# A mixture-of-experts layer on one core: the experts' output goes into a transposed residual in SBUF, column by column, in place of rows scattered to memory

## The reference

```python
h = rmsnorm(x, g_moe)                       # 512 x 1024
top_val, top_idx = top_k(h @ w_router + b_router, 4)      # 32 experts
gate = softmax(top_val)
# for each token and each of its 4 experts e:
hc  = h[tok] @ w1[e] + b1[e]                # 1024 -> 2048
act = glu * sigmoid(1.702 * glu) * (lin + 1)
y   = act @ w2[e] + b2[e]                   # 1024 -> 1024
out[tok] += gate * y
x = x + out
return rmsnorm(x, g_final)
```

## Time and profile before

| | us |
|---|---|
| median of three runs | 1723.14 |
| profiled execution, whole | 1722.98 |
| its span, first to last instruction | 1721.3 |
| PE busy | 1642.4 (95%) |
| DVE / ACT / POOL busy | 579.2 / 480.6 / 218.8 |
| DMA, mean over the span | 293 GB/s, 505.08 MB |

### The profile page before, as it was taken

One profiled execution on the slowest core, in us unless ns is written; L12 is line 12 of the kernel. 1 busy time (PEld: TensorE's weight loads), 2 busy tenths in 40 slices (PEclk: granted clock), 3 DMA queues, 4 the chain that ended last, 5 costly groups with the idle time before them and its releaser, 6 DMA issues.

```text
span 1721.3 us, 41456 instructions
## 1 busy us (share of the span) xinstructions
PE 1642.4 (95%) x15736; PEld 933.8 (54%) x15736; DVE 579.2 (34%) x1893; ACT 480.6 (28%) x1534; POOL 218.8 (13%) x719
## 2 busy tenths in 40 slices
PE   7989999999999999799999999999999999999985
PEld 6756887788889858534343434343434334333341
DVE  4344525534645351652132213221312122131115
ACT  5465332443325342312121212121211212112111
POOL 0011301000000001012121202220211112012010
PEclk9999999999999999999999999999999999999998
DMA  7202634324225506699999999999999999999996
GB/s 249 74 25 57 218 130 170 101 88 158 98 98 177 201 14 245 228 398 374 416 417 420 419 419 419 421 418 420 419 420 419 420 420 420 420 420 419 419 401 268
DMA packets 97419, 505.08 MB, mean 293 GB/s; under 512 B 9744, under 2 KB 9928, under 8 KB 47760
## 3 DMA queue, kind: packets, MB, share of 16 engines
q1 hardware_dynamic: 87808, 473.99, 68.8%
q0 software_dynamic: 8880, 26.70, 4.6%
q10 hardware_dynamic: 576, 2.10, 0.3%
HBM read 477.86 MB, written 25.03 MB: 292 GB/s over the span
## 4 chain that ended last, share of the span: by engine, by line
PE 73%; SPq 14%; DMA 7%; DVE 2%; issue 2%; ACT 1%; POOL 0%; DVEq 0%; POOLq 0%; ACTq 0%; another core or an unknown queue 0%
PE ps L2060 20%; SPq L547 13%; PE ps L2086 11%; PE ps L1711 10%; PE ps L1712 10%; PE ps L1713 10%; DMA ring<-in_w_exp_in 3%; DMA ring<-in_w_exp_out 2%; PE ps L1807 1%; DMA ring<-y_tok 1%; PE ps L1854 1%; PE ps L1874 1%; PE ps L2023 1%; DMA r_rows<-work 1%; PE ps L515 1%
## 5 line engine op out<-in xcount | busy, mean ns | idle before, releaser
L2060 PE MATMUL ps<-ring,moe 128*32 128x512 f32 x3104 | 344.2, 593 | 14.7 <-DMA ring<-in_w_exp_in 14.7
L1575 DVE TENSOR_SCALAR moe<-ps 128x768 f32<-128x768 f32 (+1 forms) x32 | 26.7, 833 | 609.3 <-PE ps L2060 609.3
L2060 PEld LDWEIGHTS ps<-ring,moe 128*32 128x32 f32 x3104 | 94.2, 110 | 247.4 <-issue 203.9
L1167 DVE TENSOR_TENSOR wl<-raw,wh 128x1024 fp32r<-128x1024 f32 x102 | 123.5, 1223 | 231.6 <-ACT wh L812 231.6
L2086 PE MATMUL ps<-ring,moe 128*32 128x256 f32 x3136 | 174.7, 379 | 0.5 <-DMA ring<-in_w_exp_out 0.3
L812 ACT ACTIVATE wh<-raw 128x1024 fp32r<-128x1024 f32 x102 | 106.9, 1060 | 224.0 <-PE ps L1713 224.0
L1711 PE MATMUL ps<-oph,wh 128*128 128x512 f32 x384 | 151.7, 395 | 4.6 <-DVE opl L1202 2.2
L1712 PE MATMUL ps<-opl,wh 128*128 128x512 f32 x384 | 150.7, 392 | 0.0
L527 DVE COPY moe<-work 128x8 f32 x960 | 127.8, 180 | 67.6 <-issue 66.7
L1713 PE MATMUL ps<-oph,wl 128*128 128x512 f32 x384 | 150.5, 392 | 0.0
L1079 ACT ACTIVATE moe<-ps 128x768 f32<-128x768 f32 (+1 forms) x32 | 22.8, 711 | 453.6 <-DVE moe L1575 453.6
(11 more groups left out here) (310 smaller groups left out, 1929.7 us busy)
## 6 DMA issues: line engine op xcount, KB each, us to landing
ring<-in_w_exp_in SPq DMA_DIRECT2D x152, 1024.0 KB
ring<-in_w_exp_out SPq DMA_DIRECT2D x78, 1024.0 KB
moe<-in_w_exp_in SPq DMA_DIRECT2D x52, 1024.0 KB
work<-in_w_exp_in SPq DMA_DIRECT2D x52, 1024.0 KB
moe<-in_w_exp_out SPq DMA_DIRECT2D x26, 1024.0 KB
raw<-in_w_in SPq DMA_DIRECT2D x25, 1024.0 KB
work<-in_w_exp_out SPq DMA_DIRECT2D x24, 1024.0 KB
y_tok<-spare POOLq DMA_DIRECT2D x16, 512.0 KB, 4.1
```

The source lines that it names most:

```text
L1167: nc.vector.tensor_tensor(half_lo(g), raw[:, g // 2 % RAW, g % 2 * PC:(g % 2 + 1) * PC], half_hi(g), ALU.subtract).then_inc(w_lo, 1)
L1575: nc.vector.tensor_scalar(act_n[:, 0:g], ps[:, 0:g, 256:512].rearrange("p j (n a) -> p j a n", a=2), 1.0 - LIMIT, 1.0 + LIMIT, ALU.max, AL ...
L2060: ins = nc.tensor.matmul(ps[32 * s:32 * s + 32, j, :], xt[:, k, 32 * j:32 * j + 32], w[:, s, :, :], start=False, stop=(k == KT - 1), tile_ ...
```

## The change

`acc_t`, the residual in transposed form (8 x 512 values in each partition), stays in `work` at 4096 to 8191. ACT writes it while it copies out the router's transposes of `res`, which are made in either version. The two weight places there go: `SLOTS` is 18, and the chunks 17 and 18 now wait for the first expert's gather (`xt_made`). `h_rows`, `r_rows`, `y_tok`, their stores and loads, the gather and the scatters are gone. The gain of the norm is applied by ACT when it writes columns, no longer by DVE to the rows.

For each expert: `y_evict` multiplies by the gate (one instruction for each group); PE transposes the result in `y_turn`, inside the `up` of two steps later, after its first chunk, through banks 6 and 7; ACT keeps it (`y_cols_keep`); DVE adds its 96 or 64 columns, each to `acc_t[:, :, token]`, ahead of `swiglu(p)`. Empty rows are filled with tokens that the expert does not have, at gate 0. ACT and POOL share the token copies half and half (48 or 32 each); DVE has none. At the end PE transposes `acc_t` back into PSUM, adds the last expert's rows there, and ACT and DVE normalise from PSUM.

```diff
-SLOTS = FIRST + 4
+SLOTS = FIRST + 2
-TURN = 5
+TURN = 3
@@ SP
                 elif s == FIRST:
-                    sp.wait_ge(nat_ready, TT)
-                    sp.wait_ge(lg_done, 1)
-                elif s == FIRST + 2:
-                    sp.wait_ge(h_stored, 16 * TT)
-                    sp.wait_ge(xt_made, 1)
+                    sp.wait_ge(xt_made, 2)
-                if s in (13, 15):
...
-                    sp.dma_start(r_rows[:, :, 512 * half:512 * half + 512], res[:, :, 512 * half:512 * half + 512]).then_inc(res_moved, 16)
+            for q in range(2, W2):
+                refill(0, W1 + q, down_chunk(0, q))
...
-            sp.dma_start(res, r_rows).then_inc(res_moved, 16)
-            sp.wait_ge(w_used, DP + down_chunk(NE - 2, W2))
-            sp.wait_ge(y_stored, scattered(NE - 1))
-            for u in range(TT * TOPK):
-                sp.dma_start(y_rows[u], y_tiles[u // TOPK, u % TOPK]).then_inc(row_in[u], 16)
@@ POOL
-                if CYCLE[i] > 2:
-                    copy_tokens(mybir.EngineType.Pool, nc.gpsimd.tensor_copy, i, LOW, CAP).then_inc(x_pool, 1)
+                pool.wait_ge(row_ready, p + 3)
+                pool.sem_inc(bias_turn, 1)
+                copy_part(i, CYCLE[i])
-            def scatter(n, g):
...
@@ ACT
-            act.wait_ge(res_moved, 32)
             for k in range(KT - 2):
                 column_tile(k)
...
-                if g > 2:
-                    nc.scalar.activation(y_sb[:, 2, :], ps[:, 5, 0:256], ACT.Copy)
-                nc.scalar.activation(y_sb[:, 0:2, :], ps[:, 4, :].rearrange("p (j n) -> p j n", j=2), ACT.Copy).then_inc(y_kept, 1)
+                for j in range(g):
+                    a = j % 2 * 256
+                    ins = nc.scalar.activation(y_sb[:, j, :], ps[:, 4 + j // 2, a:a + 256], ACT.Copy, scale=gate_now[:, j:j + 1])
+                ins.then_inc(y_kept, 1)
...
+            def y_cols_keep(n, g):
+                act.wait_ge(yt_made, n + 1)
+                act.wait_ge(acc_done, n)
+                act.sem_inc(bias_turn, 1)
+                nc.scalar.activation(y_cols[:, 0:g * 256].rearrange("p (h n) -> p h n", h=2), ps[:, 6:8, 0:g * P], ACT.Copy).then_inc(yt_kept, 1)
@@ DVE
-                nc.vector.scalar_tensor_tensor(h_nat[:, t, :], res[:, t, :], rstd[:, t:t + 1], g_moe_b,
-                                               ALU.mult, ALU.mult).then_inc(nat_ready, 1)
+                nc.vector.tensor_scalar(h_nat[:, t, :], res[:, t, :], rstd[:, t:t + 1], None, ALU.mult).then_inc(nat_ready, 1)
...
+            def add_columns(row, g, lo, hi, step=None):
+                columns = y_cols[:, 0:g * 256].rearrange("p (h j s n) -> p s h j n", h=2, j=g, s=4)
+                for s in range(lo, hi, 8):
+                    for i, token in enumerate(load_tokens(mybir.EngineType.DVE, row, s)):
...
+                        at = acc_t[:, :, bass.ds(token, 1)].rearrange("p (s h) n -> p s h n", h=2)
+                        j, n = divmod(s + i, 32)
+                        ins = nc.vector.tensor_tensor(at, at, columns[:, :, :, j, n:n + 1], ALU.add)
...
+            def add_rows(n, g, b):
+                dve.wait_ge(row_kept, n + 1)
+                dve.wait_ge(yt_kept, n + 1)
+                dve.wait_ge(acc_done, n)
+                dve.sem_inc(bias_turn, 1)
+                add_columns(tok_acc[b], g, 0, 32 * g).then_inc(acc_done, 1)
...
-            def turn(p, i, g, stores):
+            def turn(p, i, done, g):
+                add_rows(p - 2, done, i)
                 swiglu(p, CYCLE[i], p * EC + UPS)
-                index(p + 2, CYCLE[i], i, row=True)
+                keep_row(p, CYCLE[i], i)
+                index(p + 2, CYCLE[i], i, rows=p + 1)
                 e = expert_at(p + 3)
                 choose_with(e, e, CYCLE[1 - i])
-                now(p - 1, g, stores)
-                copy_part(p + 2, i)
+                now(p - 1, g, p - 1)
@@ DVE, the end
+            add_rows(NE - 3, CYCLE[1], 1)
...
+            add_columns(tok_acc[0], CYCLE[0], 0, LOW)
             swiglu(NE - 1, CYCLE[1], DP + up_chunk(NE - 1, W1))
+            add_columns(tok_acc[0], CYCLE[0], LOW, CAP).then_inc(acc_done, 1)
@@ PE
+            def y_turn(n, g, ats, ys):
+                pe.wait_ge(at_kept, ats)
+                pe.wait_ge(y_kept, ys)
+                for h in range(2):
+                    for j in range(g):
+                        ins = nc.tensor.transpose(ps[:, 6 + h, j * P:(j + 1) * P], y_sb[:, j, h * P:(h + 1) * P], ident)
+                ins.then_inc(yt_made, 1)
...
-                up(p, CYCLE[i], p * 2 + 1)
+                up(p, CYCLE[i], p * 2 + 1, between={0: lambda: y_turn(p - 2, older, p, p - 1)})
...
-                act_turn(p, CYCLE[i])
+                act_turn(p, CYCLE[i], p - 1)
...
+            up(NE - 1, CYCLE[1], 2 * NE - 1, between={1: rows_turn})
+            act_turn(NE - 1, CYCLE[1], NE - 1)
+            last_down({t: lambda t=t: tile_back(t) for t in range(TT - 1)})
+            tile_back(TT - 1)
+            for t in range(TT):
+                own_rows(t).then_inc(own_done, 1)
```

More of the change, by code:

```diff
@@ L57 @@
 AHEAD = 5
-ROWS = 8
 W1 = KT
@@ L300, in layer_kernel @@
         g_moe_c = small[:, 0:8]
-        logit_t = work[:, 6656:7168]
+        logit_t = spare[:, 256:768]
         ss_more = xmax
@@ new lines, in _ @@
+            chain.wait()
+            dve.wait_ge(pick_ready, 1)
+            chain(nc.vector.tensor_scalar(slots[:, :, 0:NE], slot, -1.0, None, ALU.add))
+            dve.wait_ge(gate_exp, 4)
+            chain(nc.vector.reciprocal(names["grec"], names["gsum"]))
+            chain.wait()
+            chain(nc.vector.tensor_tensor(gate, gate, names["grec"].unsqueeze(2).to_broadcast([P, TT, TOPK]), ALU.mult))
+            chain.wait()
+            chain(nc.vector.tensor_tensor(oh2, oh, gate.unsqueeze(3).to_broadcast([P, TT, TOPK, NE]), ALU.mult))
@@ L1519, in _ @@
             for j in range(1, BLK):
-                chain(nc.vector.scalar_tensor_tensor(slots[:, :, j * NE:(j + 1) * NE], sel, 4.0 * T, slot, ALU.mult, ALU.add))
-            chain.wait()
-            for j in range(1, BLK):
-                v = slots[:, :, j * NE:(j + 1) * NE]
-                chain(nc.vector.tensor_scalar(v, v, -1.0 - CAP * j - 4.0 * T, None, ALU.add))
+                chain(nc.vector.tensor_scalar(slots[:, :, j * NE:(j + 1) * NE], slot, -1.0 - CAP * j, None, ALU.add))
             chain.wait()
@@ L1952, in _ @@
             ins.then_inc(lg_done, 1)
-            def keep_running(n):
-                for _ in range(n):
-                    nc.tensor.matmul(ps[:, 3, 0:P], ident, ident, start=True, stop=True, skip_group_check=True)
             def column_turn(k):
@@ L1973, in _, with index @@
             ins.then_inc(rank_done, 1)
-            def index(n, g, row=False):
+            def index(n, g, first=False):
                 pe.wait_ge(pick_ready, n + 2)
-                pe.wait_ge(found_out, n)
-                if row:
-                    if n > 2:
-                        pe.wait_ge(row_ready, n - 2)
-                    for t in range(TT):
-                        for c in range(2):
-                            nc.tensor.matmul(ps[0:1, 3, 64:64 + 32 * g], column[:, t, c, 0:1], pick[:, t, 0:32 * g],
-                                             start=(t == 0 and c == 0), stop=(t == TT - 1 and c == 1), skip_group_check=True)
+                if not first:
+                    pe.wait_ge(found_out, n)
+                    pe.wait_ge(row_ready, n)
+                for t in range(TT):
+                    for c in range(2):
+                        nc.tensor.matmul(ps[0:1, 3, 64:64 + 32 * g], column[:, t, c, 0:1], pick[:, t, 0:32 * g],
+                                         start=(t == 0 and c == 0), stop=(t == TT - 1 and c == 1), skip_group_check=True)
                 for t in range(TT):
@@ L2089, in down, with last_down @@
                     ins.then_inc(w_used, 1)
-            def last_down():
+            def last_down(between={}):
                 pe.wait_ge(at_kept, NE)
@@ L2155, in _ @@
                                            start=(t == 0), stop=(t == TT - 1))
-            ins.then_inc(xt_made, 1)
+                if k % 4 == 3:
+                    ins.then_inc(xt_made, 1)
             pe.wait_ge(b_hi, 3)
             pe.wait_ge(ht_out, 2 * KT)
-            index(0, groups(0))
-            up(0, groups(0), 1, first=True, between={1: lambda: index(1, groups(1))}, kept=1)
-            x_turn(1)
-            index(2, CYCLE[0], row=True)
-            act_turn(0, groups(0), 2)
@@ L2164, in _ @@
-            up(1, groups(1), 3, kept=2)
+            pe.wait_ge(tok_ready, 1)
+            up(0, groups(0), 1, first=True, between={0: lambda: index(0, groups(0), first=True), 3: lambda: index(1, groups(1))})
+            index(2, CYCLE[0])
+            act_turn(0, groups(0))
+            up(1, groups(1), 3)
             spread(0, groups(0), 0, 3, 0)
-            index(3, CYCLE[1], row=True)
+            index(3, CYCLE[1])
```

(10 more changed lines are left out.)

560 lines of the change are left out of this document (225 added, 335 removed).

## The result

The changed kernel takes 1741.86 us (median of four runs, 1739.7 to 1746.78) against 1722.57 us before (four runs as well): the ratio is 1.0111, 95% interval 1.0097 to 1.0125. The forecast was 1698 us. The profiled execution has a span of 1744.9 us, 23.6 more than before.

A forecast was written before the change was run, and what follows sets the result against it. The prediction took the expert loop as a race, PE eating the lead of loaded chunks, then DMA pacing from about 1270 us. Terms -5.1 + 12.2 - 19.6 - 3.5 - 9.2 = -25.2 gave span 1696.1, time 1698 us, range 1691 to 1703 (50%).

The forecast's parts named there:

- Transfers: Weight loads in the expert loop: DMA needs 60.1 us a pair without scatters, 1.45 more than PE; lead 24 us.
- signs of being wrong: Expert loop: adds' batches over 1.86 us, PE waiting for weights before 1600, or pairs staying at 60 us or more.
- the end: After the last `up`: 37.8 us to the end of the span in place of 47.0, a gain of 9.2 us.
- The hand-over: From routing to the first expert: no store of `res`, gather 5.9 us earlier; net -5.1 us, first weight product about 714.
- Rival 3: The hand-over gives nothing, as copies of expert 1's columns or another gather wait hold it up: +5, 1703 us; 10%.
- `y_turn`: PE's added transposes in each `up`: a pair becomes 58.65 us; +12.2 us up to the end of `up(18)`.
- DVE's adds: DVE's column adds ahead of `swiglu`: 0.205 us a column, hidden by `down` up to 0.232 in three-group steps.
- Rival 2: DVE paces the loop: adds at 0.2485 us a column give 1724 us, at 0.262 1744 us; 15%.
- The lead: Weight chunks loaded ahead at the first expert: worth 24 us in place of 34; PE should just not run dry.
- Rival 1: DMA still paces the loop, as scatters cost only their bytes: 60.8 us a pair, 1705 to 1710 us; 18%.

The follow-up runs named there:

- e5: e4 with the loop's first instruction 64 places behind a block's start in place of at it: 1740.11 us, ratio 1.0096 to the kernel before.
- e4: Changed kernel, all adds kept, with 16 tokens a read in place of 8 and VectorE's loop put at a block's start: 1704.32 us, ratio 0.9878.
- e2: Changed kernel with every second add of VectorE left out, all token reads kept: 1697.20 us, ratio 0.9845 to the kernel before.
- e8: e4 with the chunk of one place in eighteen loaded as two transfers, of 120 and 8 partitions: 1846.58 us, ratio 1.0703.

## Why the prediction was wrong, by its own steps

**The step that failed is *Transfers*: "Without scatters the DMA engines need 60.1 us for a pair".** It took the 419 GB/s of the earlier trace rows for a property of the transfers and put it beside a new program. In these runs the rate held only while all sixteen engines had queued work. VectorE's body went from 180 to 392 instructions, and queue 14 began to fetch it, 5 packets of 8 KB a pair, and one engine fell behind with them. Between 940 and 1070 us the 16th landing fell behind the 15th by (22.1 - 6.1) - (9.5 - 3.0) = 9.5 us, 7.3 in 100, while 11 packets came: 0.9 us for each fetch, where the packet itself lasts 0.325 us. Once the lead of the others is used up, all go at the pace of the late one: 418 less 7.3% is 388 GB/s, and 392 was measured. 25.17 MB at 392 take 64.2 us; the pairs took 64.9, where the prediction had 60.1 for DMA and 58.65 for PE. Two of its own signs of being wrong came: PE waits for weights before 1600 (from 1177 us on), and pairs stay over 60 us.

The share of 1.01 in the earlier trace rows hid the risk, and the prediction priced the adds by VectorE's time alone. How many instructions a loop has is a cost of its own, and it was nowhere among the terms, nor in the rivals. The profile of the kernel before shows that such fetches exist, 29 packets on queue 14 in the whole run, and that its loop causes none; what a longer body would do can't be read there. The Trainium skill, Runtime: NRT & Kernel Launch, section "Instruction fetch mechanics", says that instruction memories are refilled by DMA in 16 KiB blocks, that the cost of crossing a block's boundary is mostly hidden, and that a taken branch to a block no longer held forces a fetch and stalls the engine. That a loop's body is fetched again agrees with the runs. The block does not: queue 14's packets are of 8 KB. Nor does the place of the cost: it lies on the DMA engine that carries the fetches (35.8 us between e5 and e4). VectorE itself pauses for 0.3 us within a batch of adds, 3 us ahead of the next packet (rows below), and e4's loop has no such pause; its slack hides them, for up to 1157 us a pair takes 58.9 us in both kernels.

**The other terms, read in e4**, where the fetches are gone (spans 1702.7 against 1721.3: -18.6, forecast -25.2):

| stretch | forecast | e4 | changed kernel |
|---|---|---|---|
| to the end of `up(18)` | -5.1 + 12.2 = +7.1 | +12.2 (1275.54 against 1263.37) | +18.9 |
| `up(18)` to `up(30)` | -19.6 | -17.7 (353.8 us) | +15.0 (386.6 us) |
| `up(30)` to `up(31)` | -3.5 | -2.7 | -2.5 |
| the end | -9.2 | -10.3 (36.6 us) | -7.8 (39.1 us) |
| sum | -25.2 | -18.5 | +23.6 |

- *The hand-over* was right in kind and too small. The first weight product starts at 713.0 us in the changed kernel and 713.5 in e4, against 720.99; 714 was forecast. Rival 3 is refuted.
- *`y_turn`*: 58.96 a pair in e4, 58.65 forecast.
- *DVE's adds* were priced right. In the changed kernel, in order of time:

```profile
1049.09 1.08 DVE L1429 TENSOR_TENSOR work<-work,spare 128x8 f32 x8 [5.18 <-issue]
1050.75 1.08 DVE L1429 TENSOR_TENSOR work<-work,spare 128x8 f32 x8 [0.58 <-issue]
1052.42 0.43 DVE L1429 TENSOR_TENSOR work<-work,spare 128x8 f32 x3 [0.58 <-issue]
1053.15 0.69 DVE L1429 TENSOR_TENSOR work<-work,spare 128x8 f32 x5 [0.30 <-issue]
...
1057.77 1.08 DVE L1429 TENSOR_TENSOR work<-work,spare 128x8 f32 x8 [0.59 <-issue]
1059.43 1.08 DVE L1429 TENSOR_TENSOR work<-work,spare 128x8 f32 x8 [0.59 <-issue]
```

1.66 us a batch, 0.208 a column (0.205 forecast, margin 0.232), with one address computation each; eight adds of 0.176 us lie within 1.08 us, so they overlap as the copies do. The batch in two parts, 3 and 5 with 0.30 us between, is one of the pauses; queue 14's next packet comes at 1056.2. Rival 2 is refuted as the cause in the loop. That its upper case, 1744 us, lies beside the measured 1741.86 is chance: it wanted 0.262 us a column. The rival holds in one place that the sum passed over: the steps of experts 2 and 3 follow experts of three groups both, so 96 columns stand ahead of a two-group step too. PE waits there 2.0 us for `swiglu`, and the end of `up(4)` is level with before (863.51 against 862.6), though the first product was 7.5 us earlier. Half the adds (e2) end `up(4)` at 858.0. Those 5.5 us are about what is missing in the first row of the table (5.1), and most of the 7.1 us between e2 and e4; that they are the same microseconds is argued from their size.
- *The lead* lasted: e4 never waits for weights, with 18 places and DMA at 419. The estimate "just not dry" stands; in its DMA arithmetic only the rate was wrong for the changed kernel.
- *The end*: 36.6 us in e4 for 37.8 forecast.
- *Rival 1* (DMA still paces) named the right resource and a wrong reason, too little saved by the scatters' going, and so 1705 to 1710. e4 refutes the reason: its transfers are those of the changed kernel, and PE never waits for them.

With the failed step mended the kernel is at 1704.3, one us outside the forecast's own range of 1691 to 1703, and faster than before, as forecast.

## What to carry to other kernels

When a change adds instructions to a loop, count the body against the instruction store before pricing them by their time (here three blocks of 128 for VectorE), and look in the profile whether an instruction queue moves packets inside the loop. If it does, shorten the body or put its start at a block's start. When DMA paces a kernel and its rate is a few per cent under what it was, compare the landings of one transfer: if one of the sixteen is always last, the mean share of the engines says nothing of the one that counts.

## What the runs showed of the hardware that was not expected

- VectorE's loop body of 382 instructions causes no fetches in the loop when it begins at a block's start, and 5 fetches of 8 KB in each pass when it begins 64 places later (e4, e5); 392 instructions cause them in either place; bodies of 180 and 232 don't where they happened to lie.
- One fetch of 8 KB sets its DMA engine back by about 0.9 us (an estimate from 9.5 us for 11 packets), three times the packet's own 0.325 us.
- In these kernels one DMA engine came to be 20 to 22 us behind the first before the rate suffered. In the changed kernel the fetches of the loop set in at some 890 us, the rate falls from about 1060 on, and PE first waits for weights at 1177.
- Queue 8, an instruction queue too, moves packets of 16 KB all the time, 2.1 MB in the run, in either kernel. That they are PE's is argued: 10 of them for 100 us are one for each 256 of the some 2,500 products and weight loads that PE executes in that time. Half of the engines fall behind the others slowly, which may be these packets' doing, by 1.5 to 2 us for 100 us, and the last landing reached 18.7 us behind the first at 1600 in the kernel before. Whether a longer run would come to the same limit wasn't tried.
- Splitting one chunk in eighteen into 120 and 8 partitions took the rate from 420 to 352 GB/s at a share of 1.01 (e8).
